# Dilated attention: two heads of a class taken as one unit, their products issued in turn

## The reference, cut to what matters

```python
ATTN_GROUPS = ((128, 1), (512, 4), (2048, 16))
...
for g, (window, dilation) in enumerate(ATTN_GROUPS):
    o, l = dilated_window_attention(q[:, :, g], k_sh[:, :, g], v_sh[:, :, g], window, dilation)
    outs.append(o)
    lses.append(l)
wts = jax.nn.softmax(jnp.stack(lses, axis=0), axis=0)
o = jnp.sum(wts[..., None] * jnp.stack(outs, axis=0).astype(jnp.float32), axis=0).astype(h.dtype)
return o.reshape(B, S, O_WIDTH) @ w_o
```

## Time and profile before

| what | value |
|---|---|
| median of the runs | 3533.27 us (3529.2 to 3545.81, three runs) |
| profiled execution, span from first to last instruction | 3530.0 us |
| mean granted TensorE clock | 0.971 |
| TensorE matmul, busy | 3327.5 us (94%) |
| VectorE, busy | 1944.8 us (55%) |
| ScalarE, busy | 1391.3 us (39%) |

### The profile page before, as it was taken

The page is one execution under the profiler, slowest core; times in us unless marked ns, Lnnn a source line. Parts: engine busy times, 40 slices in busy tenths (PEclk is TensorE's granted clock), DMA queues, the critical chain, the costliest instruction groups (busy, mean ns, idle before and its releaser), DMA issues.

```text
span 3530.0 us, 42246 instructions
## 1 busy us (share of the span) xinstructions
PE 3327.5 (94%) x14912; PEld 2604.5 (74%) x14912; DVE 1944.8 (55%) x3038; ACT 1391.3 (39%) x2064; POOL 396.0 (11%) x241
## 2 busy tenths in 40 slices
PE   8899999998999989999988999999999999999998
PEld 6667777676777777888866888877887767668886
DVE  5765777567557765545374544465354443465353
ACT  4453566444536664222223222232223444432121
POOL 3101122330012223000000000010001000010000
PEclk9999999999999999999998999999999999999999
DMA  3101699321017993223313222323232212023232
GB/s 124 45 1 60 220 321 321 123 75 34 12 61 254 323 310 102 86 95 92 99 41 91 72 97 93 101 84 130 90 100 103 90 36 72 25 66 102 89 100 73
DMA packets 174980, 389.60 MB, mean 110 GB/s; under 512 B 11312, under 2 KB 70064, under 8 KB 174192
## 3 DMA queue, kind: packets, MB, share of 16 engines
q1 hardware_dynamic: 173424, 377.45, 32.9%
q0 software_dynamic: 1408, 10.23, 0.8%
HBM read 381.34 MB, written 6.29 MB: 110 GB/s over the span
## 4 chain that ended last, share of the span: by engine, by line
PE 68%; DVE 13%; DMA 8%; ACT 4%; DVEq 3%; issue 2%; POOL 1%; POOLq 0%; ACTq 0%; SPq 0%
PE ps L549 19%; PE ps L551 18%; PE ps L550 18%; DMA gate_up_stage<-in_w_gu 8%; DVE moe_lo L1907 4%; PE ps L699 3%; PE ps L666 2%; ACT moe_hi L1113 2%; PE ps L721 2%; PE ps L705 1%; PE ps L803 1%; PE ps L769 1%; ACT w_hi L1113 1%; PE ps L657 1%; DVE w_lo L1537 1%
## 5 line engine op out<-in xcount | busy, mean ns | idle before, releaser
L1537 DVE TENSOR_TENSOR w_lo<-w_stage,w_hi 128x1024 fp32r<-128x1024 f32 (+3 forms) x310 | 398.4, 1287 | 850.1 <-ACT w_hi L1113 849.2
L549 PE MATMUL ps<-xs_hi,w_hi 128*128 128x512 f32 (+2 forms) x1952 | 778.5, 399 | 45.5 <-DVE w_lo L1537 15.1
L1113 ACT ACTIVATE w_hi<-w_stage 128x1024 fp32r<-128x1024 f32 (+3 forms) x350 | 382.1, 1093 | 1023.9 <-PE ps L551 1010.4
L551 PE MATMUL ps<-xs_hi,w_lo 128*128 128x512 f32 (+2 forms) x1952 | 772.2, 396 | 0.0
L550 PE MATMUL ps<-xs_lo,w_hi 128*128 128x512 f32 (+2 forms) x1952 | 771.8, 395 | 0.0
L549 PEld LDWEIGHTS ps<-xs_hi,w_hi 128*128 128x128 f32 (+2 forms) x1952 | 369.2, 189 | 147.3 <-issue 28.0
L551 PEld LDWEIGHTS ps<-xs_hi,w_lo 128*128 128x128 f32 (+2 forms) x1952 | 369.1, 189 | 85.6
L550 PEld LDWEIGHTS ps<-xs_lo,w_hi 128*128 128x128 f32 (+2 forms) x1952 | 370.0, 190 | 83.2
L1907 DVE TENSOR_TENSOR moe_lo<-gate_up_stage,moe_hi 128x1024 fp32r<-128x1024 f32 x224 | 270.0, 1248 | 116.9 <-ACT moe_hi L1113 116.7
L1113 ACT ACTIVATE moe_hi<-gate_up_stage 128x1024 fp32r<-128x1024 f32 x224 | 226.1, 1054 | 139.4 <-DMA gate_up_stage<-in_w_gu 131.9
L551 PE MATMUL ps<-h_hi,w_lo 128*128 128x512 f32 x704 | 278.1, 395 | 0.0
(11 more groups left out here) (366 smaller groups left out, 5006.7 us busy)
## 6 DMA issues: line engine op xcount, KB each, us to landing
gate_up_stage<-in_w_gu SPq DMA_DIRECT2D x112, 1024.0 KB, 5.5
w_stage<-in_f_gu SPq DMA_DIRECT2D x174, 512.0 KB, 3.5
down_stage<-in_w_dn SPq DMA_DIRECT2D x112, 512.0 KB, 5.8
w_stage<-in_f_dn SPq DMA_DIRECT2D x64, 704.0 KB, 4.0
w_stage<-in_w_in SPq DMA_DIRECT2D x30, 512.0 KB, 3.7
w_stage<-in_d_qk SPq DMA_DIRECT2D x24, 512.0 KB, 3.5
w_stage<-in_w_out SPq DMA_DIRECT2D x16, 512.0 KB, 3.6
w_stage<-in_d_v SPq DMA_DIRECT2D x12, 512.0 KB, 3.5
```

Source lines behind the costliest of these rows:

```text
L549: pe.matmul(o, lh, rh, start=start, stop=False)
L551: return pe.matmul(o, ll, rh, start=False, stop=stop)
L1113: copy = lambda o, i: nc.scalar.activation(o, i, ACT.Copy)
L1537: tt(w_lo[:, s, 0:n], stage[:, s, 0:n], w_hi[:, s, 0:n].bitcast(F32), ALU.subtract).then_inc(w_split, 1)
```

## The change

A pair, the two heads of one class, becomes the unit: four pairs in a call. The two heads' score products are issued in turn (512 columns of head 0, 512 of head 1, then 128 and 128, then 128 and 128), head 0 into banks 2 and 3, head 1 into 4 and 5. The transposes stay one head at a time, in banks 6 and 7. The two heads' mix products are issued in turn into the two partition halves of one bank, and one copy and one subtraction over 128 partitions take them out. `d_prob` gets four buffers, `d_prob_t` four; of the added ones all but one lie over the tiles of squares, temporaries and rotated heads. TensorE's order is now: scores of pair 0, idle products, scores of pair 1, and then for each pair p the transposes of its first head, the mix of pair p-1, the transposes of its second head, the scores of pair p+2. The core of the diff:

```diff
         def units_d(e):
-            for h in range(2):
-                r = slice(64 * h, 64 * h + 64)
-                for c in range(4):
-                    cols = slice(c * P, c * P + P)
+            for c in range(4):
+                cols = slice(c * P, c * P + P)
+                for h in range(2):
+                    r = slice(64 * h, 64 * h + 64)
...
-        D_BANKS, D_RING = (2, 4), 3
+        D_S, D_T, D_O = (2, 4), 6, (0, 1)
...
+        def wide_out(pair):
+            return ps[:, D_O[pair % 2], 0:P]
...
(TensorE)
+                def pair_scores(p):
+                    both = [U[2 * p], U[2 * p + 1]]
+                    for i in range(3):
+                        for h in range(2):
+                            k, at = both[h]["keys"][i]
+                            o = wide_scores(h)[:, at:at + k.shape[-1]]
+                            last = pe.matmul(o, both[h]["q"][i], k, start=True, stop=True)
+                            if i == 2:
+                                last.then_inc(s_full, 1)
+
+                def turned(n):
+                    pe.wait_ge(p_norm, d0 + n + 1)
+                    if n >= 1:
+                        pe.wait_ge(pt_copied, c0 + n)
+                    for i in range(6):
+                        last = pe.transpose(turned_bank[:, i * P:i * P + P], dprob[n % 4][:, i * P:i * P + P], ident[:, :])
+                    last.then_inc(pt_full, 1)
+
+                def pair_mix(p):
+                    pe.wait_ge(pt_copied, c0 + 2 * p + 2)
+                    if p >= 2:
+                        pe.wait_ge(o_split, d0 // 2 + p - 1)
+                    for i in range(6):
+                        for h in range(2):
+                            last = pe.matmul(wide_out(p)[64 * h:64 * h + 64, :], U[2 * p + h]["v"][i],
+                                             dprobt[(2 * p + h) % 4][:, i * P:i * P + P], start=i == 0, stop=i == 5)
+                    last.then_inc(o_full, 1)
+
+                pair_scores(0)
                 keep_clock(2, 6)
+                for p in range(-1, N + 1):
+                    if 0 <= p < N:
+                        turned(2 * p)
+                    if p >= 1:
+                        pair_mix(p - 1)
+                    if 0 <= p < N:
+                        turned(2 * p + 1)
+                    if p + 2 < N:
+                        pe.wait_ge(masked, c0 + 2 * (p + 1) + 2)
+                        pair_scores(p + 2)
...
(ScalarE)
+                exps(0)
+                exps(1)
+                for p in range(N + 1):
+                    if p < N:
+                        turned(2 * p)
+                    if p + 1 < N:
+                        exps(2 * p + 2)
+                    if p >= 1:
+                        act.wait_ge(o_full, o0 + p)
+                        copy(hi_of(U[2 * p - 2]), wide_out(p - 1)).then_inc(o_hi_done, 1)
+                    if p < N:
+                        turned(2 * p + 1)
+                    if p + 1 < N:
+                        exps(2 * p + 3)
...
(VectorE)
                 mask_scores(0)
+                mask_scores(1)
+                normalise(0)
+                for p in range(N + 1):
+                    if p + 1 < N:
+                        mask_scores(2 * p + 2)
+                    if p < N:
+                        normalise(2 * p + 1)
+                    if p + 1 < N:
+                        mask_scores(2 * p + 3)
+                        normalise(2 * p + 2)
+                    if p >= 1:
+                        un = U[2 * (p - 1)]
+                        v.wait_ge(o_hi_done, d0 // 2 + p)
+                        tt(lo_of(un), wide_out(p - 1), hi_of(un).bitcast(F32), ALU.subtract).then_inc(o_split, 1)
```

More of the change, by code:

```diff
@@ L194, in build_program @@
         mask_d = sb("mask_d", [P, NT, T + 2 * P])
-        dprob, dprobt = sb("d_prob", [P, 3, 768]), sb("d_prob_t", [P, 768])
+        dprob_a, dprobt_a = sb("d_prob", [P, 3, 768]), sb("d_prob_t", [P, 768])
         dm_hi, dm_lo = sb("d_mix_hi", [P, 4, T], F32R), sb("d_mix_lo", [P, 4, T], F32R)
@@ L201, in build_program @@
         w2_hi, w2_lo = sb("w_ahead_hi", [P, 2, W_FULL], F32R), sb("w_ahead_lo", [P, 2, W_FULL], F32R)
+        dprobt_b = sb("d_prob_t1", [P, 768])
+        dprob = [dprob_a[:, i, :] for i in range(3)] + [over(at_sums, "d_prob3", [P, 768], at=4096)[:, :]]
+        dprobt = [dprobt_a[:, :], dprobt_b[:, :], over(at_tmp, "d_prob_t2", [P, 768])[:, :], over(at_rot, "d_prob_t3", [P, 768])[:, :]]
         FOUR_HI = [w2_hi[:, 0, :], w2_hi[:, 1, :], w_hi[:, 0, 0:W_FULL], w_hi[:, 1, 0:W_FULL]]
@@ L338, in build_program, with wide_scores @@
         S_BANKS, S_RING = (2, 3, 1), 4
-        D_BANKS, D_RING = (2, 4), 3
+        D_S, D_T, D_O = (2, 4), 6, (0, 1)
+        def wide_scores(n):
+            b = D_S[n % 2]
+            return ps[:, b:b + 2, :].rearrange("p b t -> p (b t)")
+        turned_bank = ps[:, D_T:D_T + 2, :].rearrange("p b t -> p (b t)")
+        def wide_out(pair):
+            return ps[:, D_O[pair % 2], 0:P]
         KEY_TILES = [(0, 1, 2), (3, 4, 5), (6, 7)]
@@ L752, in attend_wide @@
             def attend_wide(U, c0):
-                N, d0 = len(U), c0 - L * UNITS
-                for n in range(2):
-                    scores(U[n], n, D_BANKS)
-                keep_clock(2, 6)
[L758 to L771, removed]
+                N, d0 = len(U) // 2, c0 - L * UNITS
@@ L1068, in two_pairs @@
                         if p2 + e > 0:
-                            pe.wait_ge(o_split, p2 * 16 + 8 * e)
+                            pe.wait_ge(o_split, p2 * 8 + 4 * e)
                         for i in range(6):
@@ L1095, in dilated @@
                     two_pairs(p2)
-                pe.wait_ge(o_split, 32)
+                pe.wait_ge(o_split, 16)
                 with_stats(SQ["dilated_out"],
@@ L1210, in attend_wide, with turned @@
             def attend_wide(U, c0, hi_of):
-                N, d0 = len(U), c0 - L * UNITS
+                N, d0 = len(U) // 2, c0 - L * UNITS
+                o0 = L * UNITS + d0 // 2
                 def exps(n):
-                    un, b = U[n], n % D_RING
+                    b = n % 4
                     act.wait_ge(masked, c0 + n + 1)
-                    nc.scalar.activation(dprob[:, b, 0:un["W"]], dprob[:, b, 0:un["W"]], ACT.Exp, bias=col[:, b, 0:1],
+                    nc.scalar.activation(dprob[b], dprob[b], ACT.Exp, bias=col[:, b, 0:1],
                                          scale=-1.0, accum_out=col[:, b, 1:2]).then_inc(p_exp, 1)
-                exps(0)
[L1221 to L1233, removed]
+                def turned(n):
+                    act.wait_ge(pt_full, c0 + n + 1)
+                    if n >= 4:
+                        act.wait_ge(o_full, o0 + n // 2 - 1)
+                    copy(dprobt[n % 4], turned_bank[:, 0:768]).then_inc(pt_copied, 1)
+                exps(0)
+                exps(1)
[11 more added lines that the diff above has]
+                        exps(2 * p + 3)
             def silu(n):
@@ L1524, in _ @@
                     attend_wide(UD[e], L * UNITS + p2 * 16 + 8 * e,
-                                lambda un: dm_hi[un["row"]:un["row"] + 64, bass.ds(2 * p2 + e, 1), un["at"]:un["at"] + P])
+                                lambda un: dm_hi[:, 2 * p2 + e, un["at"]:un["at"] + P])
             down_squares(SQ["dilated_out"], j + 19, c + 18, 4 * P, "ffn3", yd)
@@ L1730, in attend_wide @@
             def attend_wide(U, c0, hi_of, lo_of):
-                N, d0 = len(U), c0 - L * UNITS
+                N, d0 = len(U) // 2, c0 - L * UNITS
                 def mask_scores(n):
-                    b, W, bank = n % D_RING, U[n]["W"], D_BANKS[n % 2]
-                    if n >= D_RING:
-                        v.wait_ge(pt_full, c0 + n - D_RING + 1)
+                    b = n % 4
+                    if n >= 4:
+                        v.wait_ge(pt_full, c0 + n - 3)
                     hold(v, s_full, c0 + n + 1)
-                    src = ps[:, bank:bank + 2, :].rearrange("p b t -> p (b t)")[:, 0:W]
-                    V.tensor_tensor_reduce(dprob[:, b, 0:W], src, mask_d[:, U[n]["mask"], :], -U[n]["scale"], 3.0e38, ALU.add, ALU.min,
+                    V.tensor_tensor_reduce(dprob[b], wide_scores(n)[:, 0:768], mask_d[:, U[n]["mask"], :], -U[n]["scale"], 3.0e38, ALU.add, ALU.min,
@@ L1741, in mask_scores, with normalise @@
                                            col[:, b, 0:1]).then_inc(masked, 1)
-                mask_scores(0)
[L1744 to L1757, removed]
+                def normalise(n):
+                    b = n % 4
+                    v.wait_ge(p_exp, c0 + n + 1)
+                    V.reciprocal(col[:, b, 3:4], col[:, b, 1:2])
+                    v.drain()
+                    ts(dprob[b], dprob[b], col[:, b, 3:4], None, ALU.mult).then_inc(p_norm, 1)
@@ L2299, in _ @@
                     attend_wide(UD[e], L * UNITS + p2 * 16 + 8 * e,
```

(4 more changed lines are left out.)

## The result

The changed kernel takes 3478.39 us, median of four runs (3468.26 to 3482.8), against 3537.24 us for the kernel before in the same comparison: a ratio of 0.9837, 95% interval 0.9812 to 0.9861. Five more runs gave 0.9849 (0.983 to 0.9868); one of the five took 11163.94 us, for a cause that is not known, and is left out of that ratio as a slow run. The change makes the kernel some 1.5% faster.

The account below looks back on a forecast made before the run. TensorE, busy 94% of the span, was taken as the bound. Four calls gaining 10.3 us each (35.54 to 25.2) took 41 us off 3530.0, giving 3489 profiled and 3492 us as median; range 3482 to 3515.

Parts of the forecast that it names:

- the two overlaps: In the dilated attention, a pair's scores take 1.50 us and its mix 1.46 us, as one head's do; chance 0.65.
- the lower bound, 1.46 us: Time for a pair's mix if the two heads' products overlap wholly, against 2.78 us if they take turns.
- The estimate from the Trainium skill: Pair mix of 1.83 us, from a speedup of 2.38 for three column tiles; a call would take 26.1 us.
- Rivals 1 and 2: 1: mixes take turns, only scores overlap, 3513 us, chance 0.13; 2: nothing overlaps, 3533 us, chance 0.04.
- rival 3: The mix's column halves hinder each other: 4.3 or 6.0 us a pair, 3537 to 3565 us in all; chance 0.07.
- the walk: Step-by-step timing of one new dilated attention call, four pairs at full clock, from measured row times: 24.5 us.
- the 0.7 us a call that I carried: Old-order calls: 34.8 us by the same step-by-step timing, 35.54 in the trace; difference added to the new call, giving 25.2.
- the head's half-clock loss: Clock loss at the start of the first, third and fourth call, 2.3, 2.3 and 0.7 us, taken to stay.
- rival 4: In the calls, VectorE's cycle binds or shorter bursts keep half clock on longer: 3495 to 3505 us; chance 0.08.
- the 2 us for the spread of the runs: Margin added at either end of the forecast range for variation between runs, giving 3482 to 3515 us.

## Why the prediction missed

**Right: the two overlaps.** The scores of a pair take 1.50 us, as the index scores let expect. For the mix no row of before had an answer and I chose the lower bound, 1.46 us; a pair takes 1.47 (2871.02 to 2872.49). That was a choice that came out, not a reading. The estimate from the Trainium skill (TensorE: Matmul & The Clock Gate, Part 3), 1.46 x 3 / 2.38 = 1.84 us (the prediction has 1.83), is too dear here: the trace differs. By the experiments at the full clock the turn in the mix is worth 3.7 us a call (28.2 against 24.5) and the turn in the scores 3.3 us (27.87, with the idle time filled, against 24.53), each beyond the 0.4 us a pair that overlap even head by head. Rivals 1 and 2 are out; of rival 3 nothing shows, since the halves of the mix cost each other nothing.

**Right: the walk.** It gave 24.5 us and the four calls take 24.52 to 24.55.

**Wrong: the 0.7 us a call that I carried.** The walk missed them in the old order, most of them where the scores end (a wait of 1.48 us in the second call where the walk has 0.9; the fourth call has 1.13), and the prediction's reading of that call leaves out a wait of 0.40 us ahead of its first mix. The walk over the new order was exact without them. 2.8 us of gain left out.

**Wrong: "the head's half-clock loss I leave as it is: the same idle time stands ahead of it".** This is the step of the mechanism that failed. The idle time was the same (1.57 and 1.51 us), but the loss of 5.3 us went: the new kernel has the full clock in all four calls. Over all profiles, calls with idle time ahead and the first scores head by head show half clock in 17 of 22; with the first scores in turn, in 2 of 28; head by head with no idle time ahead, in none of 2. The changed kernel and its variants carry this, with 10 of 10 against 1 of 24; in the kernel before and its variants it is 7 of 12 against 1 of 4, too few to tell. So rival 4, which let the clock take some of the gain, had the wrong sign: pairing the scores gives clock back.

The terms then are 4 x (35.54 - 24.53) = 44.0 us at the full clock and 5.3 us of half clock: 49.3, where I had 41. The sum is measured; how it divides is not so sure, as both parts take the second call for all four. With 35.02 us for the first and third call and 35.19 for the fourth it would be 42.6 and 6.7.

That alone would have put the forecast at 3484, the lower end of its own range, where both terms were allowed for as bounds. What took the time below 3482 is the last term, the 2 us for the spread of the runs, and it was too small: the four runs of the changed kernel span 14.5 us, with the profiled one (3482.8) the slowest of them, and the time outside the calls differs by 24 us between profiles. A range on a median of a few such runs wants 5 us or more at either end.

What stays open: why two of the 28 calls with paired first scores still had 3.4 us of half clock, both the third call, why the fourth call of before loses in one profile and not in the other, and what it is in paired scores that kept the clock up.

## What to carry to other kernels

When a product uses half of the array, by 64 contracted rows or 64 output columns, look for its twin on the other half and issue the two in turn, in groups of two products at most (the mix alone was measured in groups): here both kinds of half took the twin for nothing. Look for a twin that already stands beside another in the trace; one row (the index scores) settled the doubt on the scores before anything was built. And when a chain at the head of a stage runs at the half clock, ask what TensorE does after its idle time as well as how long the idle time is.

## What the runs showed of the hardware

- Two output-column halves overlap as fully as two row halves: 24 matmuls in 1.53 us, as 12 before. The Trainium skill (TensorEngine Tiling (Array Packing), Key Properties) says that tiles work independently; the trace now agrees for columns too.
- TensorE starts the other half ahead of its turn, with three matmuls of the first still to start: six products a head in a row take 2.38 us in place of 2.78, and groups of two cost 0.04 us more than single ones.
- After 1.5 us of idle time, half-row products one head at a time went with the half clock in 17 of 22 calls, and the same products in turn, though busy for a shorter time (1.50 us a pair in place of 2.46 to 2.81), in 2 of 28.
